# Small 64x64 products of the RWKV part moved onto two quarters of the array, with their copies merged

## The reference

```
def step(state, inp):
    r_t, w_t, k_t, v_t, a_t, b_t = inp
    sa = jnp.einsum('bhvk,bhk->bhv', state, a_t)
    state = (state * w_t[:, :, None, :] + sa[..., None] * b_t[:, :, None, :]
             + v_t[..., None] * k_t[:, :, None, :])
    return state, jnp.einsum('bhvk,bhk->bhv', state, r_t)
```

## Time and profile before

| | |
|---|---|
| median of 3 runs | 1358.64 us (1358.18 to 1360.14) |
| the profiled execution | 1358.64 us, its span 1356.8 us |
| PE busy | 1299.1 us, 96% |
| PE weight loads busy | 1145.8 us, 84% |
| DVE busy | 890.0 us, 66% |
| ACT busy | 672.3 us, 50% |
| POOL busy | 231.2 us, 17% |
| records of the small products | 57.9 to 278.1 us |

### The profile page before, as it was taken

How to read it: one execution, slowest core, us unless ns; L and a number is a source line. 1 busy time by engine, 2 the same in 40 slices (tenths; PEclk the granted TensorE clock), 3 DMA queues, 4 the chain that set the end, 5 groups by cost and what they waited for, 6 DMA issues and landing times.

```text
span 1356.8 us, 26559 instructions
## 1 busy us (share of the span) xinstructions
PE 1299.1 (96%) x10058; PEld 1145.8 (84%) x10058; DVE 890.0 (66%) x1726; ACT 672.3 (50%) x1282; POOL 231.2 (17%) x326
## 2 busy tenths in 40 slices
PE   7999999989889999999999989999999999999997
PEld 6888998878789988999988866888888976888886
DVE  5677877747656586788746556766646665766644
ACT  4455555543246645766535446544434566544433
POOL 0002222221344311232301000122200000122200
PEclk9999999999899999999999999999999999999999
DMA  7312112114311144555555412455554622455552
GB/s 314 125 66 93 65 64 69 59 65 171 138 63 63 65 176 164 179 176 182 189 202 179 155 63 94 154 185 185 187 187 156 216 95 67 151 186 185 186 186 93
DMA packets 26771, 189.90 MB, mean 140 GB/s; under 512 B 2960, under 2 KB 3088, under 8 KB 4400
## 3 DMA queue, kind: packets, MB, share of 16 engines
q1 hardware_dynamic: 25632, 182.55, 37.3%
q0 software_dynamic: 1040, 5.96, 1.5%
HBM read 186.40 MB, written 1.05 MB: 138 GB/s over the span
## 4 chain that ended last, share of the span: by engine, by line
PE 82%; DVE 7%; ACT 5%; issue 2%; DVEq 2%; DMA 1%; POOL 1%; POOLq 0%; ACTq 0%; SPq 0%
PE ps L594 35%; PE ps L622 12%; PE ps L540 10%; PE ps L624 6%; PE ps L857 3%; DVE ring_r L1959 2%; ACT early_r L1349 1%; PE ps L706 1%; PE ps L695 1%; DMA ring<-in_weights 1%; PE ps L565 1%; PE ps L874 1%; PE ps L763 1%; ACT xn L1393 1%; PE ps L572 1%
## 5 line engine op out<-in xcount | busy, mean ns | idle before, releaser
L1426 ACT ACTIVATE w_hi<-ring 128x1024 fp32r<-128x1024 f32 x125 | 132.6, 1061 | 306.9 <-PE ps L594 163.2
L622 PE MATMUL ps<-h_both,w_hi 128*128 128x512 f32 x704 | 249.3, 399 | 0.4 <-DVE h_both L1942 0.4
L1972 DVE TENSOR_TENSOR w_lo<-ring,w_hi 128x1024 fp32r<-128x1024 f32 x125 | 155.2, 1242 | 132.9 <-ACT w_hi L1426 132.7
L624 PE MATMUL ps<-h_both,w_lo 128*128 128x256 f32 x704 | 197.7, 281 | 0.0
L594 PE MATMUL ps<-h_both,w_hi 128*128 128x256 f32 x1008 | 182.9, 284 | 0.5 <-DVE h_both L1942 0.5
L622 PEld LDWEIGHTS ps<-h_both,w_hi 128*128 128x128 f32 x704 | 132.3, 188 | 34.6 <-issue 1.2
L594 PEld LDWEIGHTS ps<-h_both,w_hi 128*128 128x128 f32 x1008 | 156.9, 192 | 3.5 <-issue 3.4
L1978 DVE TENSOR_TENSOR w_lo<-ring,w_hi 128x1024 fp32r<-128x1024 f32 x125 | 157.2, 1258 | 0.0
L540 PE MATMUL ps<-oT_r,ring_r 128*128 128x256 f32 x512 | 145.6, 284 | 0.0
L594 PE MATMUL ps<-h_both,w_lo 128*128 128x256 f32 x504 | 142.6, 283 | 0.0
L624 PEld LDWEIGHTS ps<-h_both,w_lo 128*128 128x128 f32 x704 | 133.0, 189 | 0.0
(11 more groups left out here) (425 smaller groups left out, 2886.4 us busy)
## 6 DMA issues: line engine op xcount, KB each, us to landing
ring<-in_weights SPq DMA_DIRECT2D x170, 1024.0 KB, 4.8
arena<-in_aux POOLq DMA_DIRECT2D x1, 2112.0 KB, 12.7
grow<-in_rows POOLq DMA_DIRECT2D x3, 512.0 KB, 4.1
cst<-in_consts SPq DMA_DIRECT2D x1, 1497.5 KB, 15.2
x<-in_x SPq DMA_DIRECT2D x1, 1024.0 KB, 5.0
arena<-in_swbias POOLq DMA_DIRECT2D x1, 1024.0 KB, 7.4
arena<-arena POOLq DMA_DIRECT2D x1, 1024.0 KB, 9.5
out<-xn SPq DMA_DIRECT2D x4, 256.0 KB, 2.3
```

What stands on the lines that cost most here:

```text
L622: pe.matmul(bank[:].rearrange("p (a t) -> p a t", a=2), hi, h_both[:, :, k, :], start=k == 0, stop=False)
L624: m = pe.matmul(bank[:, 0:S], lo, h_hi[:, k, :], start=False, stop=k == KT - 1)
L1426: act.activation(w_hi[:, half_of(u0, m), WH:], ring[:, (u0 + m) % RING, WH:], ACT.Copy).then_inc(w_hi_p, 1)
L1972: dve.tensor_tensor(w_lo[:, half_of(u0, m), WH:], ring[:, (u0 + m) % RING, WH:], w_hi[:, half_of(u0, m), WH:].bitcast(F32), ALU.subtract). ...
```

## The change

In `grams` and at levels 0 to 4 the Q products now write the half of PSUM that they read, like all the others. With that the crossing copies are merged: ACT's copy of Q is one instruction of 128 partitions, and DVE's masks of P and Q are two instructions of 128 partitions instead of three. The products are also put in another order. Each loop now pairs one product on the upper half with another kind of product on the lower half, in different banks, and a second loop takes the halves the other way round. At levels 1 to 3 the products with Z are woven into these loops, and Q is signalled (`pow_q`) after all 24 products instead of after 16; P is signalled (`pow_p`) after 16 as before. The numbers and shapes of the products stay.

```
@@ grams
                 for c in range(NC):
-                    for own, other in ((upper, lower), (lower, upper)):
-                        quarter(own(ps[6])[:, cols[c]], own(BK)[:, c, 0, :], own(AR)[:, c, 0, :])
-                        mm = quarter(other(ps[2])[:, cols[c]], own(AR)[:, c, 0, :], own(BK)[:, c, 0, :])
+                    quarter(upper(ps[6])[:, cols[c]], upper(BK)[:, c, 0, :], upper(AR)[:, c, 0, :])
+                    quarter(lower(ps[2])[:, cols[c]], lower(AR)[:, c, 0, :], lower(BK)[:, c, 0, :])
+                for c in range(NC):
+                    quarter(lower(ps[6])[:, cols[c]], lower(BK)[:, c, 0, :], lower(AR)[:, c, 0, :])
+                    mm = quarter(upper(ps[2])[:, cols[c]], upper(AR)[:, c, 0, :], upper(BK)[:, c, 0, :])
                 mm.then_inc(pq0_mm, 1)
@@ power_level
-                def square_q(own, other, c):
-                    return quarter(other(ps[5])[:, cols[c]], own(p_)[:, c, :], own(q_)[:, c, :])
+                def square_q(half_of_rows, c):
+                    return quarter(half_of_rows(ps[5])[:, cols[c]], half_of_rows(p_)[:, c, :], half_of_rows(q_)[:, c, :])
...
                 if lvl < 4:
                     for c in range(NC):
-                        for own, other in halves:
-                            p_last = square_p(own, c)
-                            q_last = square_q(own, other, c)
+                        square_p(upper, c)
+                        square_q(lower, c)
+                    for c in range(NC):
+                        p_last = square_p(lower, c)
+                        if lvl:
+                            times_z(upper, c)
+                        else:
+                            q_last = square_q(upper, c)
                     p_last.then_inc(pow_p, 1)
+                    if lvl:
+                        for c in range(NC):
+                            q_last = square_q(upper, c)
+                            z_last = times_z(lower, c)
+                        z_last.then_inc(z_mm, 1)
                     q_last.then_inc(pow_q, 1)
                 elif lvl == 4:
                     for c in range(NC):
-                        for own, other in halves:
-                            q_last = square_q(own, other, c)
-                            z_last = times_z(own, c)
+                        square_q(upper, c)
+                        times_z(lower, c)
+                    for c in range(NC):
+                        q_last = square_q(lower, c)
+                        z_last = times_z(upper, c)
                     q_last.then_inc(pow_q, 1)
                     z_last.then_inc(z_mm, 1)
-                if lvl in (1, 2, 3):
-                    for c in range(NC):
-                        for own, other in halves:
-                            z_last = times_z(own, c)
-                    z_last.then_inc(z_mm, 1)
-                if lvl == 5:
+                else:
                     for c in range(NC):
                         times_z(upper, c)
                         z_last = times_z(lower, c, bank=4)
@@ take_powers (ACT)
-                for own, other in ((slice(0, HD), slice(HD, P)), (slice(HD, P), slice(0, HD))):
-                    ins = act.activation(PQ[lvl % 2][own, 1].rearrange("p c t -> p (c t)"), ps[5][other, 0:S], ACT.Copy)
-                ins.then_inc(pq_ready, 1)
+                act.activation(PQ[lvl % 2][:, 1].rearrange("p c t -> p (c t)"), ps[5][:, 0:S],
+                               ACT.Copy).then_inc(pq_ready, 1)
@@ masks (DVE)
-                dve.tensor_tensor(PQ0[:, 0], ps[6][:, 0:S].rearrange("p (c t) -> p c t", c=NC),
-                                  pq[:, 0:CH].unsqueeze(1).broadcast_to((P, NC, CH)), ALU.mult)
-                for own, other in ((slice(0, HD), slice(HD, P)), (slice(HD, P), slice(0, HD))):
-                    ins = dve.tensor_tensor(PQ0[own, 1], ps[2][other, 0:S].rearrange("p (c t) -> p c t", c=NC),
-                                            pq[other, CH:P].unsqueeze(1).broadcast_to((HD, NC, CH)), ALU.mult)
+                for i, bank in ((0, 6), (1, 2)):
+                    ins = dve.tensor_tensor(PQ0[:, i], ps[bank][:, 0:S].rearrange("p (c t) -> p c t", c=NC),
+                                            pq[:, i * CH:(i + 1) * CH].unsqueeze(1).broadcast_to((P, NC, CH)), ALU.mult)
                 ins.then_inc(pq0_ready, 1)
```

More of the change, by code:

```diff
@@ L899, in power_level, with square_p, times_z @@
                 cols = [slice(c * CH, (c + 1) * CH) for c in range(NC)]
-                halves = (upper, lower), (lower, upper)
-                def square_p(own, c):
-                    return quarter(own(ps[4])[:, cols[c]], own(q_)[:, c, :], own(p_)[:, c, :])
-                def square_q(own, other, c):
-                    return quarter(other(ps[5])[:, cols[c]], own(p_)[:, c, :], own(q_)[:, c, :])
-                def times_z(own, c, bank=6):
-                    return quarter(own(ps[bank])[:, cols[c]], own(q_)[:, c, :], own(z_)[:, c, :])
+                def square_p(half_of_rows, c):
+                    return quarter(half_of_rows(ps[4])[:, cols[c]], half_of_rows(q_)[:, c, :], half_of_rows(p_)[:, c, :])
+                def square_q(half_of_rows, c):
+                    return quarter(half_of_rows(ps[5])[:, cols[c]], half_of_rows(p_)[:, c, :], half_of_rows(q_)[:, c, :])
+                def times_z(half_of_rows, c, bank=6):
+                    return quarter(half_of_rows(ps[bank])[:, cols[c]], half_of_rows(q_)[:, c, :],
+                                   half_of_rows(z_)[:, c, :])
                 if lvl < 4:
                     for c in range(NC):
-                        for own, other in halves:
-                            p_last = square_p(own, c)
-                            q_last = square_q(own, other, c)
-                    p_last.then_inc(pow_p, 1)
+                        square_p(upper, c)
[6 more added lines that the diff above has]
+                            q_last = square_q(upper, c)
+                    p_last.then_inc(pow_p, 1)
+                    if lvl:
[3 more added lines that the diff above has]
+                        z_last.then_inc(z_mm, 1)
                     q_last.then_inc(pow_q, 1)
```

## The result

The changed kernel takes 1369.08 us in the median of 4 runs (1368.37 to 1369.26), the kernel before, run beside it, 1358.41 us (1355.39 to 1360.14). The ratio is 1.0084, with a 95% interval of 1.0066 to 1.0100: 9.0 to 13.6 us slower. The ratio is that of the fast executions: 20 of the changed kernel, 1366.37 to 1373.80 us, without two slow ones of 1454.33 and 7242.45 us. The prediction was 15.6 us slower, with a range that began at 1370, so the direction was right and the size too large. The profiled execution after took 1370.71 us, its span is 1368.9 us, 12.1 above the span before.

A forecast was written before the change was run, and what follows sets the result against it. The prediction took TensorE (PE) to bound the RWKV part; its terms 1.49 + 1.95 + 8.17 + 1.70 + 2.33 = 15.6 us, added to 1358.64, gave 1374.3 us. The range was 1370 to 1380 us.

The forecast's parts named there:

- The bound: RWKV part: PE is the bound, with one short wait a phase; a microsecond of added PE work costs one outside waits.
- Two quarters instead of four: Grams and levels 0 to 4: products take 58 ns instead of 29, 0.47 us a block, 22.4 us for eight pairs.
- The count of blocks: Phase-by-phase sum: each grown block adds 0.47 us; phase 6 was said to have no grams and given five blocks, +2.33 us.
- The waits freed: Before the third chunk's state product, phases 0 to 4: PE's waits for ACT shrink, freeing 0.85 + 3.03 = 3.9 us.
- predicted remainder of 0.12: Phase 0, before the third chunk's state product: the 0.97 us wait falls to about 0.12 us.
- Phase -1: Grams(0) and levels 0 to 2 add 1.87 us, ACT's chain gets 0.38 shorter, levels 3 and 4 hide: +1.49 us.
- Phase 5: PE's waits of 0.45 and 0.65 us for DVE's L2210 both go: 2.80 - 1.10 = +1.70 us.
- Phase 6: No grams, PE is the chain to the end of level 5: levels 0 to 4 add 5 x 0.47 = +2.33 us.
- Masks: DVE's masks: two of 64 x 256 become one of 128 x 256, 0.42 us less a pair; nothing waits, counted as nothing.
- clock: TensorE: one 3.4 us half-rate stretch more or less costs at most 1.7 us, 1372.6 to 1376.0; with the forecast, chance 0.84.
- rival B: PE's waits for ACT all stay, so +22.4 us, 1381.0 us; chance 0.09 including what lies between it and the forecast.
- Predicted credit: Phases -1 to 5: waits and shorter ACT chain offset part of the 22.4 us, including 3.9 in phases 0 to 4.

The follow-up runs named there:

- the wait alone taken out: Kernel before with one ScalarE edit: third chunk's copy of U moved ahead of the second half of the weight cast; 1350.78 us against 1354.68, ratio 0.9971.
- U's copy first: Changed kernel with the third chunk's copy of U moved ahead of the second half of the weight cast; 1370.77 us, ratio 1.0089 to the kernel before.
- grams alone: Kernel before with only the raw P and Q of grams on two straight quarters and DVE's masks merged; 1361.21 us against 1358.50, ratio 1.0012.
- extra products: Kernel before with eight small products done twice at three places, in phases 3, 5 and -1; one execution each, 1352.94 us beside 1357.23.

## Why the prediction was wrong, point by point

- **The bound.** Right: PE bounds phases 0 to 4 and 6, and 0.47 us more in phase 3 costs 0.47 us.
- **Two quarters instead of four.** Right, mechanism and size: "I take 0.47 a block" was 0.46; 48 blocks give 22 us. The Trainium skill (TensorEngine Tiling, Tile-to-Partition Mapping) lists four tiles in the 64x64 mode, one for each pair of halves. The trace agrees: 0.62 us on four of them against 1.08 on two for the same 16 products. The Trainium skill (TensorE: Matmul & The Clock Gate, Part 3, The mechanism) states that a weight load overlaps running products only where the row group differs. That makes no difference here: the block takes 0.62 us with neighbours on one row group and 0.63 with alternating ones.
- **The count of blocks.** The sum holds 47 grown blocks, not 48: grams(7) is missing, 0.47 us. Put right, it moves the forecast to 1374.7 us, further from the measured time.
- **The waits freed.** This step failed, in the words "What is freed is 0.85 + 3.03 = 3.9 us". Two sizes in it were wrong. The wait was taken as the recorded idle, 0.75 us, where the starts show 1.02 (0.95 in the kernel with the wait alone taken out, of which 0.08 is still left there); and the relief of ACT's chain as the duration of a copy, 0.38 us, where the chain got 0.70 shorter. With 0.38 a wait of 0.19 us would have remained in phases 1 to 4 (1.02 - 0.45 - 0.38) and none did. The two measured sizes fit phase 0 too: there the wait had cost 1.22 us (from level 3 to level 4 4.61 us before; without any wait 3.84 in the changed kernel with U's copy first, less the 0.455 of its grown block) where 0.97 was recorded, and 1.22 - 0.455 - 0.70 leaves 0.07, where the experiment found 0.09. That this is near the predicted remainder of 0.12 is luck, as two errors cancel. Measured, the block behind the wait moves by -0.56 instead of -0.29 us in each of phases 1 to 4 and by -0.68 instead of -0.38 in phase 0, 1.4 us in all.
- **The end of a phase.** Not in the prediction. Before, the next grams started 0.33 us after the last dense product (phase 2), after the change 0.21; the profile records no idle for either. DVE's last sum ended just ahead of it before, so it is the likely releaser:

```profile
170.66 0.43 DVE L2205 TENSOR_TENSOR arena<-ps,arena 64x256 f32<-64x256 f32 x1
```

  In phase 2 of the kernel before, of the one with the wait alone taken out and of grams alone, grams starts 0.14 to 0.15 us after this sum ends, while the distance to the last dense product is 0.33, 0.41 and 0.33. After the change it is 0.21, the distance where PE waits for nothing. No experiment moved this sum by itself. That is another 0.12 us in each of phases 1 to 4. In phase 0 it is the other way round: that end grew by 0.15, in the changed kernel and with grams alone, and there the sum now ends 0.15 ahead of grams. With the wait (4 x 0.27), the end of the phase (4 x 0.12) and 24 blocks that grew by 0.455 instead of 0.467 it accounts for 1.84 of the 1.85 us by which these phases came out cheaper.
- **Phase -1.** Wrong the other way: "it gets 0.38 shorter and levels 3 and 4 hide beside it". ACT's chain got shorter, but PE was late next: after, the chain of waits runs on PE through levels 3 and 4 and the bonus products behind them (L846, L823), the last of which releases DVE's L2167 at 80.84. Grams(0) and levels 0 to 2 cost their full 0.46 each, as predicted; what the shorter ACT chain gave back was spent on levels 3 and 4, and the phase grew by 1.86 instead of 1.49.
- **Phase 5.** The recorded idle of 0.45 and 0.65 us was taken as all that could be hidden, 1.10; measured 2.73 - 0.82 = 1.9 us are hidden. The chain of waits after shows why:

```profile
245.24 0.38 PE ps L956 x2
...
253.14 0.49 PE ps L966 x2
```

  From the scan's first product to L966 it is 7.90 us through DVE; before, from 235.27 to 243.18, 7.91. (L966 after is the scan's L958 before.) Two grown blocks lie beside it and cost nothing. If each of the two waits had cost 0.26 us more than recorded, as the waits for ACT did, they would account for 1.62 of the 1.9 us; that is an estimate, and where the rest was hidden stays open.
- **Phase 6.** Six blocks grew by 2.73 us and the time by 2.40, so 0.3 us was hidden, nearly all of it between levels 0 and 1. The prediction hid nothing there; that its +2.33 is close to the measured number is luck, since the missing grams(7) made up for it.
- **Masks, clock, rival B.** The masks gave nothing, as said. Rival B is refuted, since the waits went. The clock shows in single runs, below.

Predicted credit: 6.3 us against 22.4 us of added PE work, and 0.5 more by the block left out. Measured: 8.7 against 48 x 0.455 = 21.8. The range was too narrow on that side because I had bounded the added work from two sides, but not the credit, and had left no room for the spread of single executions (1355.39 to 1360.14 us for the kernel before).

## What to carry to other kernels

Small products pay by the quarter of the array: count for each quarter how many products it gets, and don't give up two of four quarters to spare a copy on an engine that isn't the bound. Price a wait by the starts on both sides of it, compared with the same place in a phase that doesn't wait, not by the recorded idle; and price a shorter chain by the starts of its instructions, not by their durations. The cure for a short wait is often the order on the engine that releases it: one line moved was worth 3.9 us.

## What the hardware showed that was not expected

- Recorded idle was 0.25 to 0.27 us below what PE lost at a wait for ACT, in two kernels (0.75 against 1.02 and, in phase 0, 0.97 against 1.22; 0.28 against 0.54). 0.16 of it is that the recorded end of a dense product lies behind the start of the next one (0.28 us long, 0.12 apart), 0.10 that the products behind a pause start further apart (0.32 or 0.33 instead of 0.22). In the changed kernel the weight load of the state product starts 0.11 us before it, behind the pause both start together.
- On ScalarE, copies of 128 partitions started 0.26 us apart while lasting 0.40; the next instruction behind a copy of 64 partitions started 0.38 to 0.41 later, and a crossing copy 0.42 behind that of P.
- The granted clock early in the program differs between executions of nearly the same work. Between 25 and 33 us, first a run at a mean of 0.66 of full speed (the kernel with U's copy first), then one at full speed (extra products):

```profile
25.00:33.00 8.00, 7.54 (x47) 7.38 (x47) 5.47 (x10) 5.73 (x10) 0.00 (x0) 0.66 0.34 139
```

```profile
25.00:33.00 8.00, 7.01 (x60) 6.89 (x60) 5.57 (x10) 5.74 (x10) 0.00 (x0) 1.00 0.33 134
```

  The edited lines start later than that in both. The first RWKV block begins at 58.56 us in the one and at 55.83 in the other, so 2.7 us of difference between single runs come from there. The nine profiled executions fall into three groups: mean clock 1.00 and first block at 55.8 to 55.9 us (three), 0.79 and 57.5 to 58.2 (four, the kernel before and the changed one among them), 0.66 and 58.6 (two). Why an execution falls into one group is open.
